# Transposes on row halves in four attentions, low ranks in halves behind the delta rule's updates, and two transposes moved to a group's start

## The reference, cut to what matters

```
def attend(q, k, v):
    s = jnp.einsum('bqhgd,bkhd->bhgqk', q, k).astype(jnp.float32)
    p = jax.nn.softmax(s, axis=-1).astype(v.dtype)
    return jnp.einsum('bhgqk,bkhd->bqhgd', p, v)
...
    w_log = (w0 + jnp.einsum('btdr,drc->btdc', jnp.tanh(wl...), w2))
    decay = jnp.exp(-jnp.exp(-jax.nn.softplus(-w_log) - 0.5))
    a = jax.nn.sigmoid((a0 + jnp.einsum('btdr,drc->btdc', al..., a2)))
...
    def step(S, inp):
        r, w, k, v, kk, a = inp
        S = (S * w[:, :, None, :]
             - jnp.einsum('bhvk,bhk->bhv', S, kk)[..., None] * (kk * a)[:, :, None, :]
             + v[..., None] * k[:, :, None, :])
        return S, jnp.einsum('bhvk,bhk->bhv', S, r)
```

## Time and profile before

| | |
|---|---|
| median of 3 runs | 2490.42 us (2487.32 to 2491.92) |
| the profiled execution's own time | 2487.92 us |
| its span | 2486.1 us, mean granted clock 0.994 |
| busy: PE, PEld, DVE, ACT, POOL | 96%, 77%, 69%, 43%, 15% of the span |
| chain that ended last, by engine | PE 83%, DVE 8%, issue 3%, ACT 3%, DMA 1% |

### The profile page before, as it was taken

How to read it: one execution, slowest core, us unless ns; L and a number is a source line. 1 busy time by engine, 2 the same in 40 slices (tenths; PEclk the granted TensorE clock), 3 DMA queues, 4 the chain that set the end, 5 groups by cost and what they waited for, 6 DMA issues and landing times.

```text
span 2486.1 us, 45211 instructions
## 1 busy us (share of the span) xinstructions
PE 2385.2 (96%) x17410; PEld 1922.4 (77%) x17410; DVE 1712.9 (69%) x2826; ACT 1062.8 (43%) x1748; POOL 380.5 (15%) x350
## 2 busy tenths in 40 slices
PE   6999999998888999999999999989999999999998
PEld 4888888866776878888788888767888885678877
DVE  3877787666565787778887763687777324776666
ACT  4232224356444622322523222475556334656354
POOL 2000001022444200000100001101002711211052
PEclk9999999999999999999999999999999999999999
DMA  7655663210000365566465553315564222113311
GB/s 294 225 194 191 194 201 125 93 39 3 4 4 19 104 215 194 192 194 203 144 216 193 191 176 99 109 38 161 186 184 138 90 97 91 31 52 128 117 45 52
DMA packets 89012, 324.76 MB, mean 131 GB/s; under 512 B 9888, under 2 KB 11040, under 8 KB 88096
## 3 DMA queue, kind: packets, MB, share of 16 engines
q1 hardware_dynamic: 86768, 310.15, 38.3%
q0 software_dynamic: 2096, 12.55, 1.5%
HBM read 321.49 MB, written 1.18 MB: 130 GB/s over the span
## 4 chain that ended last, share of the span: by engine, by line
PE 83%; DVE 8%; issue 3%; ACT 3%; DMA 1%; DVEq 1%; POOLq 0%; POOL 0%; ACTq 0%; SPq 0%
PE bank L522 20%; PE bank L523 20%; PE bank L524 20%; PE bank L532 5%; PE bank L533 3%; PE bank L1519 1%; DVE row_statistics L1577 1%; PE bank L1548 1%; PE bank L1530 1%; DMA projections<-stream_k 1%; DVE weights_hi_lo L427 1%; DVE work L1602 1%; PE bank L2414 1%; PE bank L1969 1%; PE bank L531 1%
## 5 line engine op out<-in xcount | busy, mean ns | idle before, releaser
L422 ACT ACTIVATE weights_hi_lo<-weight_ring 128x1024 fp32r<-128x1024 f32 (+1 forms) x338 | 352.2, 1042 | 992.0 <-PE bank L524 933.9
L522 PE MATMUL bank<-input_hi,weights_hi_lo 128*128 128x512 f32 (+1 forms) x1688 | 643.2, 381 | 12.3 <-DVE input_lo L866 4.5
L427 DVE TENSOR_TENSOR weights_hi_lo<-weight_ring,weights_hi_lo 128x1024 fp32r<-128x1024 f32 (+1 forms) x333 | 403.4, 1211 | 351.4 <-ACT weights_hi_lo L422 349.8
L523 PE MATMUL bank<-input_lo,weights_hi_lo 128*128 128x512 f32 (+1 forms) x1688 | 639.8, 379 | 0.0
L524 PE MATMUL bank<-input_hi,weights_hi_lo 128*128 128x512 f32 (+1 forms) x1688 | 639.5, 379 | 0.0
L522 PEld LDWEIGHTS bank<-input_hi,weights_hi_lo 128*128 128x128 f32 x1688 | 318.8, 189 | 79.0 <-issue 16.0
L524 PEld LDWEIGHTS bank<-input_hi,weights_hi_lo 128*128 128x128 f32 x1688 | 318.8, 189 | 59.6
L523 PEld LDWEIGHTS bank<-input_lo,weights_hi_lo 128*128 128x128 f32 x1688 | 318.8, 189 | 59.3 <-issue 0.7
L806 POOL TENSOR_TENSOR work<-work 128x512 f32<-128x512 f32 (+1 forms) x48 | 68.4, 1426 | 1225.2 <-ACT work L691 1224.3
L598 DVE CUSTOM_DVE_ANT_0 work<-weight_ring,extra_tiles 128x1024 f32<-128x1024 f32 x176 | 224.5, 1275 | 35.8 <-issue 13.2
L522 PE MATMUL bank<-hidden_hi_lo,weights_hi_lo 128*128 128x512 f32 x632 | 246.8, 390 | 0.0
(11 more groups left out here) (598 smaller groups left out, 3725.2 us busy)
## 6 DMA issues: line engine op xcount, KB each, us to landing
weight_ring<-stream_k SPq DMA_DIRECT2D x481, 512.0 KB, 3.4
weight_ring<-stream_f SPq DMA_DIRECT2D x64, 448.0 KB, 3.4
weight_ring<-stream_f SPq DMA_DIRECT2D x32, 512.0 KB, 3.7
projections<-stream_k SPq DMA_DIRECT2D x14, 512.0 KB, 6.5
extra_tiles<-condrows POOLq DMA_DIRECT2D x3, 1024.0 KB, 8.2
constants<-consts POOLq DMA_DIRECT2D x1, 2112.5 KB, 8.3
residual_stream<-xin SPq DMA_DIRECT2D x1, 2048.0 KB, 10.4
work<-nabias POOLq DMA_DIRECT2D x1, 2048.0 KB, 9.3
```

The costliest lines, as they stand in the source:

```text
L422: act.activation(split_place(place)[:, 0, 0:words], w[:, 0:words], ACT.Copy).then_inc(hi_ready, 1)
L427: eng.tensor_tensor(split_place(place)[:, 1, 0:words], ring[:, n % RING, 0:words], split_place(place)[:, 0, 0:words].bitcast(F32), ALU.sub ...
L522: pe.matmul(out, weights[:, 0, w], x_hi, start=first, stop=False)
L523: pe.matmul(out, weights[:, 0, w], x_lo, start=False, stop=False)
```

## The change: what it does, and the diff

1. In all four attentions a 128x128 transpose becomes two of 64 rows each: the moving operand is the upper or lower 64x64 part of the identity, the stationary one 64 rows of the probabilities. The two alternate between banks 4 and 5, so that a bank now holds the 64 columns of one row half for both heads. ScalarE's copy reads them in that order and writes them through `crossed`, which puts the two halves beside each other again, and the mixes read the result under a flat index. 352 transposes become 704.
2. In groups 0 to 2, levels 0 to 2, the low rank is two matmuls of 256 columns, the first behind the update of unit 0 and the second behind that of unit 1. The one of level 3 stays where it was.
3. In group 3 the two bonus sums are split and placed the same way.
4. At the start of groups 1 to 3 the transposes of the first unit's first two factors come ahead of its first products, together with the waits that they need, and the wait on the copied inputs (`inputs_copied`) comes behind them.

```diff
--- before.py
+++ after.py
@@ -1476,7 +1476,8 @@
 
         def attention_turned(which, u):
 
-            return BIG[:, 16 + u % 2 * 2:18 + u % 2 * 2, :] if which == "odd" else WORK[:, 20 + u % 2 * 2:22 + u % 2 * 2, :]
+            two = BIG[:, 16 + u % 2 * 2:18 + u % 2 * 2, :] if which == "odd" else WORK[:, 20 + u % 2 * 2:22 + u % 2 * 2, :]
+            return two.rearrange("p b t -> p (b t)")
 
         def mix_bank(which, u):
 
@@ -1525,9 +1526,12 @@
                     pe.wait_ge(probs_scaled, u0 + u + 1)
                     if u >= 1:
                         pe.wait_ge(turned_copied, u0 + u)
+                    nt = len(key_tiles(which, pairs[u][1]))
                     for b in range(2):
-                        for i in range(len(key_tiles(which, pairs[u][1]))):
-                            mm = pe.transpose(pb[4 + b][:, tok(i)], attention_probs(which, u)[:, b, tok(i)], C("ident"))
+                        for i in range(nt):
+                            o = slice((b * nt + i) * HD, (b * nt + i + 1) * HD)
+                            for h, half in enumerate(HALF):
+                                mm = pe.transpose(pb[4 + h][:, o], attention_probs(which, u)[half, b, tok(i)], C("ident")[half, half])
                     mm.then_inc(probs_turned, 1)
                 u = it - 3
                 if 0 <= u < n:
@@ -1546,7 +1550,8 @@
                         for b in range(2):
                             ch = attention_operands(which, t, b, qt)[2]
                             mm = pe.matmul(mix_bank(which, u)[HD * b:HD * b + HD, 0:P], attention_values(which, tile, ch),
-                                           attention_turned(which, u)[:, b, tok(i)], start=i == 0, stop=i == len(keys) - 1)
+                                           attention_turned(which, u)[:, tok(b * len(keys) + i)], start=i == 0,
+                                           stop=i == len(keys) - 1)
                     mm.then_inc(mixed, 1)
                     if which == "odd" and u == n - 1:
                         odd_out_half(pe, 1, range(KT - 1))
@@ -1637,7 +1642,8 @@
                     act.wait_ge(probs_turned, u0 + u + 1)
                     if u >= 2:
                         act.wait_ge(mixed, u0 + u - 1)
-                    act.activation(attention_turned(which, u)[:, :, 0:nk], banks[:, 4:6, 0:nk], ACT.Copy).then_inc(turned_copied, 1)
+                    act.activation(crossed(attention_turned(which, u)[:, 0:2 * nk]),
+                                   banks[:, 4:6, 0:nk].rearrange("p h (i c) -> p h i c", c=HD), ACT.Copy).then_inc(turned_copied, 1)
                 if which == "odd" and it in ODD_SLAB_BESIDE:
                     odd_slab_hi(act, ODD_SLAB_BESIDE[it])
                 if it < n:
@@ -2266,10 +2272,14 @@
                 wkv_ends_tensor(pe, g)
             wkv_scan_tensor(pe)
 
-        def bonus_sum(pe, j):
+        def bonus_sum(pe, j, part=None):
 
             pe.wait_ge(readout_made, j // 2 + 1)
-            pe.matmul(pb[6 + j % 2][:, :], C("blk"), BONUS_KEYS[:, j, :], start=True, stop=True).then_inc(bonus_summed, 1)
+            for cols in (ALL,) if part is None else (((0, TC), (TC, T))[part],):
+                c = slice(*cols)
+                mm = pe.matmul(pb[6 + j % 2][:, c], C("blk"), BONUS_KEYS[:, j, c], start=True, stop=True)
+            if part != 0:
+                mm.then_inc(bonus_summed, 1)
 
         def out_gate(pe, j):
 
@@ -2313,7 +2323,7 @@
             pe.matmul(pb[a][:, :], S("a2", low.start, low.stop, j * P, P), BIG[low, AL, :], start=True, stop=True)\
               .then_inc(lora_ready, 1)
 
-        def wkv_low_rank(pe, n, part):
+        def wkv_low_rank(pe, n, part, cols=ALL):
 
             low, j = slice(HD * (n // 4), HD * (n // 4) + HD), n % 4
             if part == n % 2:
@@ -2321,8 +2331,10 @@
             else:
                 pe.wait_ge(sigmoids_ready, n - 1 - n % 2 + part)
             weights, ranks = (("w2", WL), ("a2", AL))[part]
-            pe.matmul(pb[7][:, :], S(weights, low.start, low.stop, j * P, P), BIG[low, ranks, :], start=True, stop=True)\
-              .then_inc(lora_ready, 1)
+            c = slice(*cols)
+            mm = pe.matmul(pb[7][:, c], S(weights, low.start, low.stop, j * P, P), BIG[low, ranks, c], start=True, stop=True)
+            if c.stop == T:
+                mm.then_inc(lora_ready, 1)
 
         def wkv_start_tensor(pe, g):
             n0, n1 = 2 * g, 2 * g + 1
@@ -2365,13 +2377,15 @@
                 mm.then_inc(kv_ready, 1)
 
             if g:
+                pe.wait_ge(group_added, 2 * g - 1)
+                pe.wait_ge(factors_ready, n0 + 1)
+                turn(n0, 0, 4)
+                turn(n0, 1, 5)
                 pe.wait_ge(inputs_copied, 2 * g - 1)
             within(n0)
             if g:
-                pe.wait_ge(group_added, 2 * g - 1)
-            for i in range(3):
-                if g and i == 2:
-                    pe.wait_ge(group_added, 2 * g)
+                pe.wait_ge(group_added, 2 * g)
+            for i in range(2 if g else 0, 3):
                 turn(n0, i, 4 + i)
             if g:
                 pe.wait_ge(inputs_copied, 2 * g)
@@ -2448,15 +2462,17 @@
                 if g == 2:
                     for s in STEPS_BETWEEN[li]:
                         wkv_step_tensor(pe, 0, s)
-                if g < 3 and li < 4:
+                if g < 3 and li == 3:
                     wkv_low_rank(pe, 2 * g + 2 + li % 2, li // 2)
-                if g == 3 and li in (1, 2):
-                    bonus_sum(pe, li - 1)
                 for u in range(2):
                     q = NLEV * g + 2 * li + u
                     pe.wait_ge(x_copied, q + 1)
                     pe.wait_ge(turned_copied_back, q + 1)
                     (update if li < LAST else turned_update)(u).then_inc(z_ready, 1)
+                    if g < 3 and li < 3:
+                        wkv_low_rank(pe, 2 * g + 2 + li % 2, li // 2, (LAT if u else CTX))
+                    if g == 3 and li in (1, 2):
+                        bonus_sum(pe, li - 1, u)
                 if g == 2:
                     for s in STEPS_BEHIND[li]:
                         wkv_step_tensor(pe, 0, s)
```

## The result

The changed kernel takes 2499.68 us (median of 11 runs, 2493.05 to 2501.14) against 2489.61 us before (11 runs, 2487.32 to 2494.63). The ratio is 1.0033, with an interval of 1.0025 to 1.0041: some 8 us slower, where the forecast had 9 us faster. On a second chip the same kernel came out at 1.0021 (1.0011 to 1.0031). The profiled execution took 2497.36 us.

What follows compares the result with a forecast made beforehand. It took a chain alternating between TensorE, VectorE and ScalarE, plus TensorE's instruction stops, as the bound. Terms 7.2 + 0.6 + 1.3 = 9.1 us gave 2478.8 for a profiled-like execution, 2481.3 as median; range 2476 to 2486.5.

Steps and rivals of the forecast that it cites:

- All three signs: Wrong if TensorE's idle before transposes grows by what they save, levels get longer, or stops exceed 8 us.
- Transposes on row halves: Four attentions: sixteen paired halves take 0.70 us against 1.03 for eight full tiles; 7.2 us faster in all.
- a third of 7.6 us comes back: Even attention: nearly all its chain parts precede TensorE work or ScalarE's copy, so 2.5 us faster.
- Low ranks in halves: Delta rule, groups 0 and 1: halves behind the updates save 0.1 us in each of six levels, 0.6 us.
- each update takes 0.51: Delta rule levels: each update keeps its traced 0.51 us with low-rank halves behind the first and second.
- GpSimd's products wait for them too: Delta rule: GpSimd's products wait for the later sigmoids, but only the next group needs them; cost nothing.
- Two transposes ahead of the first products: Group starts in the delta rule: transposes run while instruction packets come; 1.3 us faster, between 0 and 3.
- the stops for instructions grow: Rival: 374 more pairs add a 1.5 us stop per group, 6 us; gain 3, about 2487; both small-gain rivals 0.25.
- unpaired halves: Rival, attentions: sixteen halves take up to 1.42 us; 9 us slower, about 2499; slower by this or something unseen 0.04.

Runs made afterwards that it cites:

- the fillers: Five unused identity transposes a step: even and odd attention, on halves alone, 0.9994; even only, on changed kernel with GpSimd's later start, 0.9988.
- Taking away the collision: Changed kernel with one more GpSimd wait, so its third operation on the first unit's keys starts after both `decay_before`: 2492.32 us, ratio 1.0008.
- changed again: The changed kernel, unaltered, measured once more on a second chip, against the kernel before: 2495.34 us, ratio 1.0021.

## Why the prediction was wrong, point by point

The forecast was 9.1 us faster; 8 and 5 us slower came. All three signs that the prediction named for being wrong are in the changed kernel's trace: TensorE waits longer before the transposes (44.0 us on the scaling in the even, third and last attention, with its load queue, where it was 33.8), a level of group 0 takes 4.68 us (606.65 to 611.33) where it took 4.58, and the stops add up to 9.0.

- **Transposes on row halves, 7.2 us.** The operation's price was right (0.64 us for sixteen; 0.70 taken), the changed shape in the third attention cost nothing to speak of (0.65 there), and that attention gave 2.0 to 2.4 of the 2.7 forecast in the five profiled executions with halves and without a stretch at 0.50 there. In the two of the changed kernel, with 10 us at 0.50 in the window 2100 to 2200, it was 0.7 and 1.0 us longer instead. In the even and odd attention the step that failed is "a third of 7.6 us comes back" and its like: the chain share was read as if nothing else would change with it. Even in an execution with a good clock the gain was 1.2 and 0.3 us (forecast 2.5 and 1.2), within the spread of single executions, and the last attention's 0.2 (0.8). By the runs of these two attentions alone nothing came (0.9999). And the prediction had no term for the granted clock at all, though the trace before showed stretches at 0.5 in both stages. The sum of the part was 1.5 us alone; its clock fell by 0.0040, which the line through the runs of before puts at some 4 us.
- **Why the clock falls there.** In these two attentions TensorE waits for VectorE's scaling (before, its load queue 14 times in the even one and 8 in the odd one); shorter transposes are made up for by a longer wait (TensorE's matmuls waited 6.1 us on L1602 in the even attention, 534 to 586, and now wait 8.8 on L1607, 534 to 587; in the odd one, with the load queue, it was 13.7 and is 18.7). The even attention's window has 43.73 us of busy PE in 54, where it had 46.16, and 50.24 with the fillers; the clocks are 0.87, 0.97 and 1.00. At a lower clock the same work counts as more busy time (the sixteen matmuls of the mixes 1.82 us at 0.50 for 1.02), so the loss of work is larger than these numbers. One window doesn't settle it, though: the halves alone have less busy time still, 42.61 us, and a clock of 0.97 in their profiled execution. The means over all runs do: 0.9931 before, 0.9891 with the halves, 0.9934 with the fillers. That more work at that place brings the clock back is shown by them; what the chip counts is not. The waits on VectorE are at most 2.6 us each for a matmul of the even attention, where the window's clock was 0.87.
- **Low ranks in halves, 0.6 us faster.** Alone 3 us slower. Two sentences failed. The bounds for a half, 0.50 to 0.68, hold (0.63), but "each update takes 0.51" doesn't: with a product of another shape behind it an update takes 0.62, and twice 0.11 turn the small gain into a loss of 0.1 a level. And "GpSimd's products wait for them too ... so I cost them at nothing" was the expensive one: nobody waits for those products, but they meet VectorE's `decay_before` when they start later (the first one at 612.20 for 608.87; against the level's start 1.5 us later, which is the delay that the prediction itself had given the sigmoids), and TensorE waits for what stands behind that. Three times 0.9 us, and in four of five profiled executions a stretch at 0.50 behind one of these waits.
- **VectorE beside GpSimd.** `decay_before` has two inputs in SBUF and takes 1.59 us beside a GpSimd product that started first, 0.69 beside one that started second (which then takes 1.51), and 0.69 without one. The subtraction behind it has one input in PSUM and kept its 0.68: in the kernel before it starts at 613.75, inside the product of 613.45 that takes 1.51. Why the one is stretched and the other isn't, no run shows.
- **Two transposes ahead of the first products, 1.3 us.** Alone nothing. What was right is that the stops move with the number of instructions ahead. What failed is the account of them: I counted which stops lie inside the runs, and took the sum of the others as constant. Measured sums between 545 and 790 us are 8.0 (before), 8.1, 7.5, 8.0, 7.8 (the parts alone), 9.2 and 9.3 (the halves in two attentions each), 9.0 to 10.7 (parts together) and 4.8 to 6.3 (with fillers). The rival "the stops for instructions grow" named this, at 6 us and for more pairs; it was at most 2.7 us, of which 1.2 to 1.4 can be the spread between executions.
- **The sum.** Alone, the parts measure -1.5 and +1.7 us. Together they are 5 to 8 slower. Up to 2.7 us of that may be stops. Taking away the collision, and then adding the fillers, brings the changed kernel from 1.0021 over 1.0008 to 0.9988; the fillers put other instructions at the stops and raise the clock at once. The remainder of some 3 us (with an uncertainty of about as much, from four ratios) is open; the clock doesn't explain it, since in the runs of "changed again" it fell by what the parts alone add up to (0.0048; halves 0.0040, the others 0.0010). On the first chip, with 0.0066, it can have part in the 3 us between the two results: 0.0018 more, some 2 us by the line through the runs of before.
- **The rivals.** The one on the other side was unpaired halves, at about 2499 us; that is close to the measured 2499.68, by coincidence, since sixteen halves took 0.64 us and not up to 1.42. No rival had the clock, or `decay_before` beside a GpSimd product. The range ended at 2486.5.

## What to carry to other kernels

Before you shorten an operation of TensorE in a stage where it waits for another engine, look at the granted clock there: where it fell at times already (17 us at 0.50 in the profile before), less work made it fall more here (0.9931 to 0.9891 in the mean of the runs), and the gain went. When a step is moved later, follow everything that starts behind it, also what nobody waits for, and see beside which operation it comes to lie (0.69 us became 1.59 here). And in this kernel's dense runs of very short matmuls the stops on "issue" came to between 4.8 and 10.7 us, by what stood ahead, so a change of the number of instructions ahead can shift the time of a stage that it doesn't touch: compare the stops for "issue" before you credit or blame an edit, and compare two executions of the same kernel first.

## What the runs showed of the hardware that was not expected

- The stops on "issue" in one and the same stage of the program ran from 4.8 to 10.7 us in 190 us, by what stood ahead of it; 1.2 to 1.4 us of that is spread between executions of the same instructions.
- 48 transposes that do nothing, together with halves where TensorE is the bound, made the kernel faster (0.9975); 80 of them took a changed kernel from 1.0008 to 0.9988 (each ratio against the kernel before on its own chip).
- A VectorE operation of 0.69 us took 1.58 or 1.59 us in three of three places of the changed kernel beside a GpSimd product, and that product took 1.52 to 1.73 instead of 1.27.
- The 770 us of dense products from 800 to 1570 us were the same within 0.1 us in all profiled executions; what differs from one to the other lies in the sparse stages, by where the stretches at 0.50 fall in them and by the stops.
- In 97 executions of one kernel a mean clock 0.001 lower went with 1.1 us more.
